# Two Strassen-Winograd pairs in four feed-forward layers, weight sums by accumulating loads, other buffers at the joints

## The reference

```
def swiglu(x, w_gate, w_up, w_down):
    return (jax.nn.silu(x @ w_gate) * (x @ w_up)) @ w_down      # 1024 -> 2816 -> 1024

h = h + 0.5 * rms_norm(swiglu(rms_norm(h, pre_g), ...), post_g)                     # f1, f2
h = layer_norm(DN_ALPHA * h + 0.5 * swiglu_2(h, w_in, w_out), ln_g, ln_b)           # a0, a1, b0, b1
```

## Time and profile before

| | |
|---|---|
| median of 3 runs | 1622.52 us |
| lowest and highest | 1622.01, 1623.05 us |
| the profiled execution | 1622.1 us |
| its span in the profile | 1620.3 us |
| TensorE, VectorE, ScalarE, GpSimd busy | 99%, 68%, 51%, 5% |
| DMA traffic | 306.79 MB, mean 189 GB/s |

### The profile page before, as it was taken

One profiled execution on the slowest core, in us unless ns is written; L12 is line 12 of the kernel. 1 busy time (PEld: TensorE's weight loads), 2 busy tenths in 40 slices (PEclk: granted clock), 3 DMA queues, 4 the chain that ended last, 5 costly groups with the idle time before them and its releaser, 6 DMA issues.

```text
span 1620.3 us, 18778 instructions
## 1 busy us (share of the span) xinstructions
PE 1598.5 (99%) x7719; PEld 1330.9 (82%) x7719; DVE 1096.2 (68%) x1055; ACT 819.2 (51%) x857; POOL 87.8 (5%) x104
## 2 busy tenths in 40 slices
PE   9999999999999999999999999899999999999998
PEld 7888897788888788888988888788888998888886
DVE  6974656679853789637668865578546666698653
ACT  6644547655642766434654654255433435446550
POOL 0241000000000000001010000000000132000000
PEclk9999999999999999999999999999999999999999
DMA  9774674466652866544657656557355654675650
GB/s 326 210 217 148 200 234 145 163 215 208 202 193 100 282 198 198 166 151 147 235 183 229 195 178 216 164 164 226 130 208 186 204 182 145 206 246 160 197 190 26
DMA packets 222100, 306.79 MB, mean 189 GB/s; under 512 B 8896, under 2 KB 144320, under 8 KB 221888
## 3 DMA queue, kind: packets, MB, share of 16 engines
q1 hardware_dynamic: 217232, 290.29, 54.9%
q0 software_dynamic: 4416, 15.05, 3.0%
q10 hardware_dynamic: 368, 0.27, 0.1%
HBM read 304.52 MB, written 1.05 MB: 189 GB/s over the span
## 4 chain that ended last, share of the span: by engine, by line
PE 82%; DVE 11%; issue 3%; ACT 2%; DMA 1%; SPq 0%; DVEq 0%; ACTq 0%
PE bank L785 23%; PE bank L798 23%; PE bank L789 20%; DVE split L1817 6%; PE bank L735 3%; PE bank L802 3%; DVE whole L1821 2%; PE bank L881 2%; PE bank L883 2%; PE bank L884 2%; ACT split L1385 1%; PE bank L847 1%; PE bank L849 1%; PE bank L852 1%; ACT sh L1564 0%
## 5 line engine op out<-in xcount | busy, mean ns | idle before, releaser
L1817 DVE TENSOR_TENSOR split<-whole,split 128x2048 fp32r<-128x2048 f32 (+2 forms) x314 | 670.6, 2158 | 266.9 <-ACT split L1385 265.3
L1385 ACT ACTIVATE split<-whole 128x2048 fp32r<-128x2048 f32 (+1 forms) x298 | 550.8, 1871 | 219.9 <-PE bank L798 80.2
L785 PE MATMUL bank<-split,xh 128*128 128x512 f32 x1212 | 329.7, 394 | 0.0
L798 PE MATMUL bank<-split,xh 128*128 128x512 f32 x1212 | 324.8, 390 | 0.0
L789 PE MATMUL bank<-split,xl 128*128 128x512 f32 x1040 | 278.4, 389 | 0.0
L798 PEld LDWEIGHTS bank<-split,xh 128*128 128x128 f32 x1212 | 227.2, 188 | 47.9 <-DVE split L1817 0.2
L785 PEld LDWEIGHTS bank<-split,xh 128*128 128x128 f32 x1212 | 223.7, 188 | 47.5 <-issue 3.0
L789 PEld LDWEIGHTS bank<-split,xl 128*128 128x128 f32 x1040 | 195.2, 188 | 41.4
L785 PE MATMUL bank<-split,th 128*128 128x512 f32 x524 | 145.4, 396 | 0.0
L789 PE MATMUL bank<-split,tl 128*128 128x512 f32 x524 | 142.7, 391 | 0.0
L798 PE MATMUL bank<-split,th 128*128 128x512 f32 x524 | 142.2, 389 | 0.0
(11 more groups left out here) (306 smaller groups left out, 1527.8 us busy)
## 6 DMA issues: line engine op xcount, KB each, us to landing
whole<-in_ffn_w_in SPq DMA_DIRECT2D x176, 512.0 KB, 5.1
whole<-in_ffn_w_out SPq DMA_DIRECT2D x40, 1024.0 KB, 5.1
whole<-in_ret_w_in SPq DMA_DIRECT2D x24, 1024.0 KB, 5.1
whole<-in_ffn_w_gate SPq DMA_DIRECT2D x42, 512.0 KB, 4.3
whole<-in_ffn_w_up SPq DMA_DIRECT2D x42, 512.0 KB, 6.0
whole<-in_ffn_w_down SPq DMA_DIRECT2D x20, 1024.0 KB, 5.1
whole<-in_w_in SPq DMA_DIRECT2D x16, 1024.0 KB, 5.5
whole<-in_gla_w_in SPq DMA_DIRECT2D x12, 1024.0 KB, 5.8
```

The lines of the kernel that those rows point to most:

```text
L785: pe.matmul(o[:, :], tokens(0, k), whi[:, k, :], start=start and k == 0, stop=False, skip_group_check=True)
L798: ins = pe.matmul(o[:, :], tokens(0, k), wlo[:, k, :], start=False, stop=end, skip_group_check=True)
L1385: act.activation(split[s][:, 0:n], whole[r][:, 0:n], ACT.Copy).then_inc(hi.mark(i), 1)
L1817: dve.tensor_tensor(split[r][:, c0:c1], whole[r][:, c0:c1], split[s][:, c0:c1].bitcast(F32), ALU.subtract).then_inc(lo.mark(*what), 1)
```

## The change

- `FFN_STEPS` becomes two orders. f1 and f2 have `ONE_PAIR`: as before, but turn 6 before turn 4 and turn 7 before turn 3. a0, a1, b0 and b1 have `TWO_PAIRS`: pairs (3, 4) and (7, 8), products often two in a row, and their turns later.
- Two of the four weight sums of a pair, t1 and t3, are made by loads: SyncE loads B12 (1 MB) into the buffer, GpSimd waits for it and issues two accumulating loads of 512 KB (B11 for t1, B22 for t3). VectorE makes t2 and t4. In f1 GpSimd's two pairs of loads stand inside the bias loop, ahead of n == 2 and n == 6; in f2 behind the load of `pf`; in the others behind the layer's gain loads. The signs of token sums and adds change with it.
- ScalarE copies the fp32 X from the PSUM banks of the turns (`act_tokens`), four copies of 128x512, and `turn_bank` waits for them; f1 adds xh and xl in four pieces on VectorE.
- High parts are allowed one tile further (`ahead(i, 1)`), low parts up to `behind(i)`. In products VectorE's adds stand before the low parts, not behind.
- `give_ffn` gives pairs of buffers for a layer's first four tiles and last eight.

The diff, cut to its core:

```diff
-    ("product", 0, "t3"), ("tile", 7, 0), ("turn", 4),
-    ("product", 0, "b21"), ("tile", 7, 1), ("turn", 6),
-    ("product", 0, "t4"), ("tile", 8, 0), ("tile", 8, 1), ("turn", 3), ("turn", 7),
+    ("product", 0, "t3"), ("tile", 7, 0),
+    ("product", 0, "b21"), ("tile", 7, 1), ("turn", 6), ("turn", 4),
+    ("product", 0, "t4"), ("tile", 8, 0), ("tile", 8, 1), ("turn", 7), ("turn", 3),
...
+TWO_PAIRS = (
+    ("tile", 0, 0), ("tile", 0, 1), ("tile", 1, 0), ("tile", 1, 1), ("turn", 0),
+    ("token sums",),
+    ("tile", 2, 0), ("product", 0, "b11"), ("blocks",), ("tile", 2, 1), ("turn", 1), ("tile", 5, 0),
+    ("product", 0, "t1"), ("product", 0, "t2"), ("tile", 5, 1), ("turn", 2), ("p",),
+    ("product", 0, "b22"), ("product", 0, "t3"), ("tile", 6, 0),
+    ("product", 0, "b21"), ("product", 0, "t4"), ("turn", 4), ("tile", 6, 1), ("turn", 5),
+    ("product", 1, "b11"), ("turn", 3), ("tile", 9, 0),
+    ("product", 1, "t1"), ("product", 1, "t2"), ("tile", 9, 1), ("turn", 6),
+    ("product", 1, "b22"), ("product", 1, "t3"), ("tile", 10, 0), ("turn", 9),
+    ("product", 1, "b21"), ("product", 1, "t4"), ("turn", 8), ("tile", 10, 1), ("turn", 7))
...
+ORDER = {"f1": ONE, "f2": ONE, "a0": TWO, "a1": TWO, "b0": TWO, "b1": TWO}
...
-                        load_key[grp.t3], load_key[grp.b22], load_key[grp.b21] = (
-                            grp.b11 + 0.5, grp.t1 - 0.1, grp.t2 - 0.1)
+                        load_key[grp.t1], load_key[grp.t3], load_key[grp.b22], load_key[grp.b21] = (
+                            grp.b11 - 0.9, grp.t2 + 0.5, grp.t1 - 0.1, grp.t2 - 0.1)
...
+        def give_ffn(name, among, into_mixer=False):
+            first, end = at[name + "gu"][0], at[name + "d"][-1] + 1
+            slots = [s for s in range(7) if SLOT[s][0] in among and SLOT[s][1] in among]
+            lead = first + (0 if name == "f1" else 4)
+            give_slots(first, lead, [slots] * 4)
+            give_blocks(lead, end - 8, among)
+            if into_mixer:
+                closing = [[s] for s in slots if s >= 5]
+                give_slots(end - 8, end, [slots] * 2 + [range(5)] * 2 + closing + [range(5)] * (4 - len(closing)))
+            else:
+                give_slots(end - 8, end, [slots] * 8)
...
+        def ahead(i, gap=2):
...
+        def behind(i):
+            return max(i, ahead(i, 1) - 1)
...
+        def pool_sum(pool, m, i):
+            b = load_to[i]
+            dst = lanes(whole[b][:, :], 4)
+            pool.wait_ge(raw_in[b].sem, raw_in[b].of(i))
+            if sum_in[m].n:
+                pool.wait_ge(sum_in[m].sem, sum_in[m].n)
+            for src, c0 in addend[i]:
+                pool.dma_start(dst[:, :, c0:c0 + 256], src, accum_op=ALU.add).then_inc(sum_in[m].mark(i), 16)
...
             for n in range(8):
+                if n == 2:
+                    pool_sum(pool, "t1", group["f1", 0].t1)
+                if n == 6:
+                    pool_sum(pool, "t3", group["f1", 0].t3)
                 pool.wait_ge(lo.sem, lo.of(6 + n))
                 pool_bias(0, n)
...
-                if i in product_of and product_of[i][2] in SUMS:
+                if i in addend:
+                    act.wait_ge(sum_in[product_of[i][2]].sem, sum_in[product_of[i][2]].of(i))
+                elif i in product_of and product_of[i][2] in ("t2", "t4"):
                     act.wait_ge(vec.sem, vec.of("sum", i))
...
+        def act_tokens(act, nx, t):
+            for g in range(2):
+                act.wait_ge(turn_lo.sem, turn_lo.of("x", nx, t, g))
+                act.activation(xs[t][g], lanes(bank_of.get(("x", nx, t, g), bank[4])[:, :], 4), ACT.Copy).then_inc(
+                    fn.mark("xs", nx, t, g), 1)
...
         def act_lead(act, stage, four, unit):
+            if stage in ORDER:
+                act_tokens(act, stage, 0)
             if stage in ("mix", "f2"):
                 act_turn_x(act, stage, 1)
...
             act_high(act, ahead(four[1]))
+            if stage in ORDER:
+                act_tokens(act, stage, 1)
...
-            dve.tensor_tensor(xs, xh[:, :, :].bitcast(F32), xl[:, :, :].bitcast(F32), ALU.add).then_inc(
...
-                added(g, grp[g].b22, "u2", u2, bank[7], "c12")
+                    dve.tensor_tensor(u2, bank[7][:, :], u2, ALU.subtract).then_inc(vec.mark("c12", name, g), 1)
+                    lows()
```

More of the change, by code:

```diff
@@ L343, in gate_up @@
                 return [(rows(wg_, 4 * n, 4, j * 256, 256), 0), (rows(wu_, 4 * n, 4, j * 256, 256), 256)]
-            for step, *what in FFN_STEPS:
+            for step, *what in ORDER[name].steps:
                 if step == "tile":
@@ L613, in pool_gain, with pool_sums @@
                 gain_in[g % GAINS].mark(g), 16)
+        def pool_sums(pool, name):
+            for n in range(len(ORDER[name].pairs)):
+                for m, i in (("t1", group[name, n].t1), ("t3", group[name, n].t3)):
+                    pool_sum(pool, m, i)
+        def pool_sum(pool, m, i):
[6 more added lines that the diff above has]
+                pool.dma_start(dst[:, :, c0:c0 + 256], src, accum_op=ALU.add).then_inc(sum_in[m].mark(i), 16)
         def pool_program(pool):
@@ L666, in pool_program @@
                 pool_gain(pool, g)
+            pool_sums(pool, "a0")
             for g in (10, 11):
@@ L915, in pe_ffn @@
         def pe_ffn(pe, f):
-            gu, dn, name, grp = at[f.name + "gu"], at[f.name + "d"], f.name, [group[f.name, g] for g in range(len(FFN_PAIRS))]
+            order = ORDER[f.name]
+            gu, dn, name, grp = at[f.name + "gu"], at[f.name + "d"], f.name, [group[f.name, g] for g in range(len(ORDER[f.name].pairs))]
             def turn(j):
                 pe.wait_ge(vec.sem, vec.of("mult", name, j, 1))
-                if j - 1 in FFN_PAIRS:
+                if j - 1 in order.pairs:
                     srcs = [u2, s5]
-                elif j in FFN_PAIRS:
+                elif j in order.pairs:
                     srcs = [u1, c4]
@@ L970, in product @@
                     pe_product(pe, grp[g].t4, *x_block(1, 1), bank[6], False)
-            steps = FFN_STEPS
+            steps = order.steps
             if name != "f1":
@@ L975, in pe_ffn @@
                 turn(0)
-                steps = FFN_STEPS[LEAD_STEPS:]
+                steps = order.steps[LEAD_STEPS:]
             for step, *what in steps:
@@ L1493, in act_ffn @@
         def act_ffn(act, f, e):
-            gu, dn, name, grp = at[f.name + "gu"], at[f.name + "d"], f.name, [group[f.name, g] for g in range(len(FFN_PAIRS))]
+            order = ORDER[f.name]
+            gu, dn, name, grp = at[f.name + "gu"], at[f.name + "d"], f.name, [group[f.name, g] for g in range(len(ORDER[f.name].pairs))]
             def silu(j, t):
-                place = PLAIN.index(j)
+                place = order.place(j)
                 act.wait_ge(passed.sem, passed.of(spot[name, j, 1], t))
                 if place >= 2:
-                    act.wait_ge(vec.sem, vec.of("mult", name, PLAIN[place - 2], t))
+                    act.wait_ge(vec.sem, vec.of("mult", name, order.plain[place - 2], t))
                 if f.turned_raw and j == 0:
@@ L1565, in act_ffn @@
                 elif step == "product":
-                    act_high(act, ahead(spot[(name, *what)]))
+                    act_high(act, ahead(spot[(name, *what)], 1))
                     product(*what)
@@ L2126, in dve_ffn @@
                     else:
-                        dve_lows(dve, ahead(spot[name, j, n]))
+                        dve_lows(dve, behind(spot[name, j, n]))
                     if n:
@@ L2139, in dve_ffn @@
                 elif step == "product":
-                    dve_lows(dve, ahead(spot[(name, *what)]))
-                    product(*what)
+                    product(*what, lambda: dve_lows(dve, behind(spot[(name, *what)])))
                 elif step == "p" and name == "f2":
```

136 lines of the change are left out of this document (74 added, 62 removed).

## The result

The changed kernel takes 1610.64 us, median of 4 runs (1609.76 to 1612.02), against 1622.51 for the kernel before: a ratio of 0.9928, 95% interval 0.991 to 0.9945. The profiled execution took 1611.23, with a span of 1609.4. The forecast was 1608, its own range 1602 to 1614.

What follows compares the result with a forecast made beforehand. TensorE, busy 1598.5 of the 1620.3 us span, was taken to set the time. Gains of 27.6 less losses of 13.0 took 1622.1 to 1607.5 (1607.9 against the median): forecast 1608, own range 1602 to 1614, whole range 1597 to 1621.

Steps and rivals of the forecast that it cites:

- Fewer matmuls: In a0, a1, b0 and b1 a second pair makes 84 products in place of 96: 10.9 us gained.
- Joints: Into the PLE gate and b0: new buffer slots remove waits of 3.75 and 4.32 and slow clock behind: 11.5 us gained.
- Turns: Turn(4) in f1, a0, a1, b0, b1: placed later, its wait behind its multiply goes: 5.2 us gained.
- VectorE in the two-pair layers: In a1's products VectorE is busy 82.0 of 96.3 us, 85%, ScalarE 62.9; no wait of TensorE, 0 taken.
- Traffic: Two-pair layers move 6 MB more each: 256 GB/s, DMA share 0.79; nothing taken for it.
- X from PSUM: TensorE's turn of X waits for ScalarE's copies: 2.45 in f2, 1.07 in a0, together 3.5 us lost.
- f1's waits: In f1 TensorE waits 2.6 for low part 7, then 5.5 at t1 for GpSimd's late loads: 9.5 us lost.
- The landing: Time for GpSimd's two accumulating 512 KB loads to land: 6 us taken, bounds from below 4 to 16.
- Rival C: Slow accumulating loads for t1 and t3 of every pair: landing of 18 us gives 1632, even at 16.1; chance 0.08.
- Rival D: VectorE becomes the bound in two-pair layers, adds idling it a product each: 8 us lost, 1616; chance 0.10.
- Rival B: f1's wait is small, loads landing early enough or low part 7 done sooner: 1599; chance 0.22.
- Rival E: The joints into the PLE gate and b0 don't close, another wait taking their place: 1619; chance 0.06.

Runs made afterwards that it cites:

- experiment 3: Changed kernel with one pair in all six layers, a0, a1, b0 and b1 using the order of f1 and f2: 1621.32 us, ratio 0.9993.
- experiment 1: Kernel before with only the new buffer slots of give_ffn, and a thirteenth buffer for f2: 1615.69 us, ratio 0.9954.
- experiment 8: Changed kernel with X of f2 and a0 made by VectorE's adds, not ScalarE's copies from PSUM: 1607.84 us, ratio 0.9904.
- experiment 4: Changed kernel with GpSimd's accumulating loads as plain loads at the same points, sums left out, so only times count: one execution, 1607.43 us.
- experiment 5: Changed kernel with f1's loads for t1 issued ahead of the first bias load, not the third: 1602.32 us, ratio 0.9868.
- experiment 6: Changed kernel with f1's low part 7 ahead of tile 2's multiplies and sl, GpSimd's order unchanged: 1612.06 us, ratio 0.9927.
- experiment 7: Changed kernel with f1's t1 loads ahead of the first bias load and low part 7 ahead of tile 2's multiplies: 1600.95 us, ratio 0.9862.
- experiment 9: Changed kernel where, in two-pair layers, GpSimd waits for ScalarE's high part of b11 before issuing t1's loads: 1631.53 us, ratio 1.0054.
- experiment 10: Changed kernel where, in two-pair layers, GpSimd waits until TensorE has passed b11 before issuing t1's loads: 1713.64 us, ratio 1.056.
- experiment 2: Kernel before with only turns 4 and 3 placed later in the order all six layers share: 1618.09 us, ratio 0.9971.

## Why the prediction was right, point by point

The sign, the mechanism of each part and nearly all sizes came true; the time is 2.6 above the forecast and in its own range. The difference lies in one term, f1's.

*Fewer matmuls*, right: 10.9 forecast, 10.6 by experiment 3.

*Joints*, right, and shown by experiment 1 to be the buffers: 11.5 forecast, 11.6 measured over the stretches in which they lie. What the prediction didn't see is that the new slots by themselves would make f2 4.3 worse under the old order; in the change this is hidden by the other edits.

*Turns*, right: 5.2 forecast, 4.7 to 5.2 measured alone.

*VectorE in the two-pair layers*, right: forecast 82.0 of 96.3, measured 81.95 of 96.80, with no wait of TensorE. ScalarE forecast 62.9, measured 60.58. *Traffic*: forecast 256 GB/s and 0.79, measured 233 and 0.83; the share is higher for fewer bytes, which fits the 2.2 times as much that accumulated bytes cost the DMA engines. No wait came of it.

*X from PSUM*, right: 2.45 and 1.07 forecast, 2.35 and 0.97 measured; shown by experiment 8.

*f1's waits*, right in place, order and cause, but mis-sized: this is the term that failed. It was 9.5 and came to 13.1 (the 12.1 measured, and the turn(4) wait of 1.0 that went inside it). Term by term: low part 7 ended at 51.57, not 50.3, which is 1.3. Of this 0.4 is that f1 was late from its opening on; the rest is that the sums of X were done only at 45.08, so that ScalarE's `sh`, for which `sl` waits, ended at 47.04 and not at 45.7. From the end of low part 7 to the landing of t1's loads it took 9.8, not 7.2, which is 2.6: issue to landing was 8.0 (8.8 median for all 40), not 6, and the second load was issued at 53.35, not 52.4. With both, ScalarE's high part of t1 ended at 63.3, not 59.4. The pass behind it took 4.9, slow clock included, against 5.2 forecast: 1.3 + 2.6 - 0.3 = 3.6. The clock fell behind the first wait too, which the prediction didn't have, but this cost nothing: t1's pass began at 63.41 with a slower or a faster clock there (experiment 8). For the same reason it is partly luck that the second wait came out at 5.05 where "about 5" was forecast: both its ends were some 4 us later, and with the clock up it was 6.44.

The landing was worked out from plain gain loads (4.0), with a double cost kept for the upper bound only. By experiment 4 plain loads at these points take 6.2 at the median and accumulating ones 2.6 more. Experiments 5 to 7 show the cause: with both edits of f1 9.7 us come back (10.7 by the ratios).

*Rival C* did not come, and its price was wrong: the two-pair layers are covered for 22 to 25 us from the first issue, not 15, and beyond that each of a layer's two pairs loses the delay, where it counted one (experiments 9 and 10; with the loads held until b11 is passed, 103 us in all). The rule of the Trainium skill that stands with it ("DMA: Bandwidth & Descriptors", section "SWDGE vs HWDGE vs iDMA": VectorE can lock GpSimd out of building descriptors) isn't borne out here: the two accumulating loads at 52.54 and 53.35, with VectorE idle, were issued in 1.37 and 1.90, and those at 75.72 and 76.52, beside VectorE's low parts, in 1.38 and 1.90.

*Rival D* did not come: VectorE was at 85%, as forecast. Rivals B and E did not come either.

## What to carry to other kernels

A step that only issues transfers or copies still has a place in its engine's order: beyond the 11.9 us by which the change was faster, a further 14.6 lay in three such orders (GpSimd's loads behind waits that they didn't need, one low part of VectorE behind work that could wait, ScalarE's copies in front of a turn). Follow the first tiles of the next stage back to the tile that last held their buffers: if it is one of the last, the joint can wait for it however idle the engines are, as two did here. Give a load that accumulates twice the DMA time of a plain one (2.2 here), and check its cover with landing times measured in the stretch where it stands: here they ran from 5.8 to 15.2 us.

## What the runs showed of the hardware

Accumulating loads of 512 KB from DRAM took 5.8 to 12.7 us, median 8.8; as plain loads at the same points 4.1 to 9.1, median 6.2. They took 2.2 times the DMA engines' time per byte, in 3.7 times as many packets. GpSimd's issue instruction took 1.3 to 1.9 us in place of 0.75. Late or early issues beside SyncE's loads landed after 11.9 (experiment 6), 13.3 and 14.7 (a1 in experiment 9) and 15.2 (experiment 5), with the DMA engines at a mean share of 0.94, 1.16, 1.12 and 1.13; at 1.10 and 1.12 in the change's own a1 it was 10.2 and 11.5, so the share doesn't settle it.

Behind f1's waits of 3.43 and 5.05 the granted clock was at 0.50 and 0.55 over the next 5 us. Behind f2's wait of 2.19 it stayed at 1.00 in the change and was 0.66 in experiment 5 behind the same wait (the stretch to the PLE gate was 172.13 and 173.66): at this length either can happen, and it is worth 1.5 us. The length of a wait doesn't settle it in this range: behind 2.41 (experiment 1) the clock was 0.67 over 5 us, behind f1's first wait of 3.09 in experiment 9 it was 1.00, and behind the joint's 3.59 it was 0.66 in the kernel before and 0.50 in experiment 2.

```profile
372.00:377.00 5.00, 4.86 (x26) 4.12 (x27) 2.21 (x4) 4.27 (x7) 2.68 (x2) 1.00 1.11 324
...
362.00:367.00 5.00, 4.55 (x17) 4.03 (x18) 1.56 (x4) 3.74 (x6) 2.67 (x2) 0.66 0.94 305
```
